# Smaller state products, one read of the new values and a moved fill in the two chunked mixers

## The reference

```python
def step(state, inp):
    u_i, w_i, qk_i, qd_i, kd_i, cd_i = inp
    u = u_i - einsum(w_i, state)                       # the new values
    o = einsum(qd_i, state) + einsum(qk_i, u)          # queries' part, and values' part
    state = state * cd_i + einsum(kd_i, u)             # next state, 64x64 for each head
    return state, o
```

## Time and profile before

| | us |
|---|---|
| median of 3 runs (lowest to highest) | 2084.54 (2083.76 to 2085.15) |
| the profiled execution, its time | 2082.22 |
| its span | 2080.4 |
| PE busy in the span | 1964.4 (94%) |
| DVE / ACT / POOL busy | 916.8 / 473.2 / 869.6 |
| mean granted TensorE clock | 0.973 of full |

### The profile page before, as it was taken

The page is one execution under the profiler, slowest core; times in us unless marked ns, Lnnn a source line. Parts: engine busy times, 40 slices in busy tenths (PEclk is TensorE's granted clock), DMA queues, the critical chain, the costliest instruction groups (busy, mean ns, idle before and its releaser), DMA issues.

```text
span 2080.4 us, 32746 instructions
## 1 busy us (share of the span) xinstructions
PE 1964.4 (94%) x13564; PEld 1566.4 (75%) x13564; DVE 916.8 (44%) x1486; ACT 473.2 (23%) x700; POOL 869.6 (42%) x1100
## 2 busy tenths in 40 slices
PE   4997999998999999999999779899999999999995
PEld 2885777766877878778778568688888888888884
DVE  6456656645444444444443562642232322323325
ACT  4213433342212212122221420521010110101102
POOL 1565422320322223232322257445565555655554
PEclk7999999998999999999999889999999999999998
DMA  7471211212122122120220652011111111111112
GB/s 312 161 235 54 71 50 53 74 74 90 59 63 82 37 85 74 52 90 29 80 74 32 258 192 71 27 35 51 46 46 49 50 50 41 50 50 50 50 41 81
DMA packets 70494, 164.94 MB, mean 79 GB/s; under 512 B 6000, under 2 KB 31088, under 8 KB 70384
## 3 DMA queue, kind: packets, MB, share of 16 engines
q1 hardware_dynamic: 62896, 144.45, 20.9%
q10 hardware_dynamic: 7488, 18.88, 2.4%
HBM read 133.95 MB, written 29.36 MB: 78 GB/s over the span
## 4 chain that ended last, share of the span: by engine, by line
PE 56%; POOL 19%; issue 17%; DMA 3%; DVE 3%; ACT 2%; SPq 1%; POOLq 0%; DVEq 0%; ACTq 0%
PE gbank L540 36%; POOL w_hi L457 9%; POOL w_lo L461 9%; PE mbank L841 3%; PE mbank L612 2%; PE gbank L632 2%; PE gbank L557 1%; DMA fa<-in_w_ada 1%; PE mbank L752 1%; PE mbank L897 1%; PE mbank L931 1%; PE mbank L621 1%; PE gbank L841 1%; PE mbank L908 1%; DMA fa<-mix_scr 1%
## 5 line engine op out<-in xcount | busy, mean ns | idle before, releaser
L457 POOL TENSOR_TENSOR w_hi<-w_raw,zero 128x256 fp32r<-128x256 f32 (+1 forms) x528 | 385.9, 761 | 1131.5 <-PE gbank L540 937.6
L540 PE MATMUL gbank<-h_hi,w_hi 128*128 128x512 f32 x1696 | 675.0, 398 | 10.7 <-POOL w_lo L461 6.9
L540 PE MATMUL gbank<-h_hi,w_lo 128*128 128x512 f32 x1696 | 674.7, 398 | 0.0
L540 PE MATMUL gbank<-h_lo,w_hi 128*128 128x512 f32 x1696 | 670.1, 395 | 0.0
L461 POOL TENSOR_TENSOR w_lo<-w_raw,w_hi 128x256 fp32r<-128x256 f32 (+1 forms) x528 | 444.5, 872 | 10.4
L540 PEld LDWEIGHTS gbank<-h_hi,w_hi 128*128 128x128 f32 x1696 | 320.4, 189 | 92.9 <-issue 20.7
L540 PEld LDWEIGHTS gbank<-h_hi,w_lo 128*128 128x128 f32 x1696 | 320.3, 189 | 70.5 <-issue 3.4
L540 PEld LDWEIGHTS gbank<-h_lo,w_hi 128*128 128x128 f32 x1696 | 320.5, 189 | 67.6 <-issue 3.0
L1056 PE MATMUL mbank<-ra,w_hi 128*128 128x512 f32 x640 | 197.0, 389 | 0.0
L1056 PEld LDWEIGHTS mbank<-ra,w_hi 128*128 128x128 f32 x640 | 120.2, 188 | 24.9
L2066 DVE SCALAR_TENSOR_TENSOR fa<-mbank,mod,fa 128x1024 f32<-128x1024 f32 x40 | 51.3, 1283 | 169.2 <-PE mbank L1056 169.2
(11 more groups left out here) (320 smaller groups left out, 2190.4 us busy)
## 6 DMA issues: line engine op xcount, KB each, us to landing
w_raw<-in_w_tail SPq DMA_DIRECT2D x74, 512.0 KB, 3.6
fa<-in_w_ada SPq DMA_DIRECT2D x48, 512.0 KB, 5.1
w_raw<-in_w_in SPq DMA_DIRECT2D x26, 512.0 KB, 3.7
p_scr<-fa ACTq DMA_DIRECT2D x20, 512.0 KB, 2.6
w_raw<-in_w_mix SPq DMA_DIRECT2D x16, 640.0 KB, 3.9
fa<-in_xT SPq DMA_DIRECT2D x16, 512.0 KB, 7.9
fa<-p_scr SPq DMA_DIRECT2D x8, 1024.0 KB, 5.7
w_raw<-in_w_gate SPq DMA_DIRECT2D x16, 512.0 KB, 4.6
```

Of the source, the lines that this page charges most:

```text
L457: last = pool.tensor_tensor(hi[:, c], raw[:, c], zero[:, 0:1].to_broadcast([P, w]), ALU.add)
L540: mm = pe.matmul(gb[bank], w, r, start=(q == 0), stop=(q == 3 * ks - 1))
```

## The change

The products with state and into state are cut to the 64x64 blocks of each head. The queries' part moves from `to_state` into `from_state`, ahead of the new values. The new values of even and odd heads go to two different banks (mb[2] and mb[1], swapped between the two chunks), and one copy reads both. The products for both next states come ahead of those into y. One more cut of the fill, at 43, stands ahead of `heads(1, gd["ltr"])`, so that 7 of the 12 matmuls that stood ahead of it follow it; and `gated(0)` goes behind `first_blocks` on DVE.

```diff
-FILL_S1 = (10, 22, 38, 50)
+FILL_S1 = (10, 22, 38, 43, 50)
-_SUM = ["rw_s", "rw_Yd", "gd_s", "gd_Yd"]
+_SUM = ["rw_s", "gd_s", "rw_Yd", "gd_Yd"]
...
                 gates(i, FILL_S1[3])
                 pe.wait_ge(sem("gd_ltr"), at("gd_ltr", i))
                 heads(1, gd["ltr"], None, "gd_g6")
+                gates(i, FILL_S1[4])
...
+                def u_bank(e, par_):
+                    return mb[2 if e == par_ else 1]
...
-                    pe.wait_ge(sem(f"{nm}_TT"), at(f"{nm}_TT", i, 5))
-                    heads(1, b_["TT"], rhs, off=off, first=nm == "rw")
+                    pe.wait_ge(sem("gd_TT"), at("gd_TT", i, 5))
+                    for h in range(4):
+                        u_ = 256 + off // 2 + h // 2 * 64
+                        for c in chunks:
+                            pe.matmul(u_bank(h % 2, c.start // 64)[c, u_:u_ + 64], b_["TT"][c, h * 64:h * 64 + 64], rhs[c, h * 64:h * 64 + 64],
+                                      start=nm == "rw" and h < 2, stop=True, skip_group_check=True)
...
                 def from_state(par_):
...
+                    if par_:
+                        pe.wait_ge(sem("gd_Yd"), at("gd_Yd", i, 1))
+                    for nm, st, yb in (("gd", 1, 3), ("rw", 0, 2)):
+                        for t in range(2):
+                            y_ = slice(t * P + 64 * par_, t * P + 64 * par_ + 64)
+                            for r in (0, 64):
+                                q_ = ar_i[r:r + 64, t * 256 + P + 64 * par_:t * 256 + P + 64 * par_ + 64] if nm == "rw" else gd["qd"][r:r + 64, y_]
+                                pe.matmul(mb[yb][r:r + 64, y_], state[r:r + 64, st, t, r:r + 64], q_,
+                                          start=nm == "gd" and par_ == 0 and t == 0, stop=True, skip_group_check=True)
                     for st in range(2):
                         for t in range(2):
-                            w_ = par_ * 256 + st * P + t * 64
-                            last = pe.matmul(mb[1][R, st * 256 + t * P:st * 256 + (t + 1) * P], uw[:, w_:w_ + 64],
-                                             state[:, st, t, :], start=False, stop=True, skip_group_check=True)
+                            w_, u_ = par_ * 256 + st * P + t * 64, 256 + st * P + t * 64
+                            for e, r in enumerate((0, 64)):
+                                last = pe.matmul(u_bank(e, par_)[R, u_:u_ + 64], uw[r:r + 64, w_:w_ + 64], state[r:r + 64, st, t, r:r + 64],
+                                                 start=False, stop=True, skip_group_check=True)
...
                 def to_state(par_):
+                    pe.wait_ge(sem("new_u"), at("new_u", i, par_ + 1))
+                    for nm, terms, s_bank in (("rw", ((rw["tokBK"][R, 0:256], rw["u"]), (rw["tokBK"][R, 256:512], rw["tokVA"])), mb[0]),
+                                              ("gd", ((gd["kd"][R, :], gd["u"]),), gb[1])):
...
+                            for n_, (key, val) in enumerate(terms):
+                                for r in (0, 64):
+                                    hc = slice(t * P + r, t * P + r + 64)
+                                    last = pe.matmul(s_bank[r:r + 64, hc], key[:, hc], val[R, hc], start=n_ == 0,
+                                                     stop=n_ == len(terms) - 1)
+                        last.then_inc(done(f"{nm}_s", i), 1)
+                    for nm, terms, yb in (("rw", ((rw["u"], rw["rbt"]), (rw["tokVA"], rw["rkt"])), 2), ("gd", ((gd["u"], gd["qkt"]),), 3)):
+                        for t in range(2):
                             for lhs, rhs in terms:
+                                for r in (0, 64):
+                                    hc, c = slice(t * P + r, t * P + r + 64), t * P + 64 * par_
+                                    last = pe.matmul(mb[yb][r:r + 64, c:c + 64], lhs[R, hc], rhs[R, hc], start=False, stop=True,
+                                                     skip_group_check=True)
...
-                gated(0)
                 dve.wait_ge(sem("gd_qkt"), at("gd_qkt", i))
                 first_blocks("gd", gd, t64(mb[1][:, 0:256]), "gd_g6", ALU.subtract)
+                gated(0)
...
                 def new_values(par_):
-                    for nm, off in (("rw", 0), ("gd", 256)):
-                        dve.tensor_copy(u_all[R, off:off + 256], mb[1][R, off:off + 256]).then_inc(done(f"{nm}_u", i), 1)
+                    dve.tensor_copy(u_all[R, :].rearrange("p (q e c) -> p e q c", e=2, c=64),
+                                    (mbank[R, 1:3, 256:512] if par_ else mbank[R, 2:0:-1, 256:512]).rearrange("p e (q c) -> p e q c", c=64)).then_inc(done("new_u", i), 1)
```

More of the change, by code:

```diff
@@ L77 @@
                + ["rw_Ym", "gd_Ym", "+rw_gm", "+rw_k2", "rw_TT", "gd_TT"]
-               + ["rw_u", "gd_u", "+rw_bonp"] + ["rw_S"] * 4 + ["gd_S"] * 4
-               + ["+rw_ar", "+rw_ar", "+rw_km", "rw_u", "gd_u", "+rw_bm", "+rw_tl", "+rw_tl"] + ["rw_S"] * 4 + ["gd_S"] * 4
+               + ["new_u", "+rw_bonp"] + ["rw_S"] * 4 + ["gd_S"] * 4
+               + ["+rw_ar", "+rw_ar", "+rw_km", "new_u", "+rw_bm", "+rw_tl", "+rw_tl"] + ["rw_S"] * 4 + ["gd_S"] * 4
                + ["+gd_kn", "+gd_kq", "+gd_dtm", "rw_yc", "gd_o", "rw_o"]),
@@ L914, in to_state @@
                         for t in range(2):
[L915 to L922, removed]
@@ L923, in to_state @@
-                        last.then_inc(done(f"{nm}_s", i), 1)
[L925 to L929, removed]
+                            for n_, (key, val) in enumerate(terms):
[3 more added lines that the diff above has]
+                                                     stop=n_ == len(terms) - 1)
@@ L930, in to_state @@
+                        last.then_inc(done(f"{nm}_s", i), 1)
+                    for nm, terms, yb in (("rw", ((rw["u"], rw["rbt"]), (rw["tokVA"], rw["rkt"])), 2), ("gd", ((gd["u"], gd["qkt"]),), 3)):
+                        for t in range(2):
                             for lhs, rhs in terms:
-                                last = pe.matmul(mb[yb][r:r + 64, c:c + 64], lhs[R, h * 64:h * 64 + 64],
-                                                 rhs[R, h * 64:h * 64 + 64], start=False, stop=True,
-                                                 skip_group_check=True)
+                                for r in (0, 64):
+                                    hc, c = slice(t * P + r, t * P + r + 64), t * P + 64 * par_
+                                    last = pe.matmul(mb[yb][r:r + 64, c:c + 64], lhs[R, hc], rhs[R, hc], start=False, stop=True,
+                                                     skip_group_check=True)
```

## The result

The change took the kernel from 2084.85 to 2037.26 us (medians of 4 runs each; 2034.72 to 2039.29 after): ratio 0.9771, 95% interval 0.9754 to 0.9788, some 47.7 us (44 to 51). The forecast was 2039.3, range 2031 to 2052. The profiled execution took 2039.29, its span 2037.4. That is 43.0 us less than the profiled span before, and not 47.7: this execution was the longest of its four, and its blocks began at 492.3 instead of about 488.8, since ahead of them the clock stood at half for 51.2 us where it was 44.4 in the profile before.

What follows compares the result with a forecast made beforehand. TensorE's queue was taken to bound the blocks. State stage 32.7, fill around T 9.5 and clock 3.0 sum to 45.2 us off the profiled 2082.22, giving 2037.0; plus 2.3 for the median, 2039.3, range 2031 to 2052.

Steps and rivals of the forecast that it cites:

- The queue: Mixer blocks: each is a single queue of TensorE work, so its savings count in full until another engine's result is late.
- The state stage: from_state and to_state: 64x64 records at 0.030 us each save about 2.05 us a half-block, 32.7 us over sixteen halves.
- The shared bank: Query products in from_state: both row halves write one bank on different partitions without going serial; otherwise saving 7 us smaller.
- rival 2: State stage: two row halves block each other in new values or queries, 7.2 us each; 2046.5, both 2053.7; chance 0.08.
- The fill around T: Before the inversion's first level: moved fill saves 1.30 us in seven blocks, 0.4 in block 0; 9.5 us in all.
- The margins of 0.3: Around the first T: ltr and T would each be ready about 0.3 us before PE needs them.
- The one copy: new_values on DVE: one 64x512 copy takes 0.68 us, hidden by fill matmuls before to_state; costs nothing.
- The clock: Mixer blocks: both falls to half clock, 1.5 us each at to_state runs, vanish as the runs shorten; 3.0 us.
- Rival 4: State stage: quarters don't overlap, a 64x64 record costs 0.11 us like the wide one; 2145 us; chance 0.02.

Runs made afterwards that it cites:

- e3: Kernel after with the first-T part undone (cut of the fill at 43 and move of gated(0)), state stage alone: 2047.80 us, ratio 0.9825, 79.55 us a block.
- e5: Kernel after with the query products in from_state as wide as before, at their new place: 2044.94 us, ratio 0.9800.
- e6: Kernel after with the products into the states as wide as before: 2052.16 us, ratio 0.9834.
- e7: Kernel after with the new values' products as wide as before, all in one bank: 2046.98 us, ratio 0.9810.
- e2: Kernel after with gated(0) back ahead of first_blocks on DVE, the cut at 43 kept: 2035.73 us, ratio 0.9771.
- e4: Kernel after with the 10 fill matmuls between from_state(0) and to_state(0) moved behind to_state(0): 2042.11 us, ratio 0.9805.
- e9: Kernel before with only the first-T part (cut of the fill at 43, gated(0) behind first_blocks): 2076.12 us, ratio 0.9957.
- e10: Kernel before, unchanged, run again for a second profile: 2086.61 us.
- e11: Kernel before, unchanged, run once more for a third profile: 2088.59 us.
- e8: Kernel after with to_state's products reordered, all of one array quarter before the other's within each group: 2045.29 us, ratio 0.9806.
- the second measurement: The same two kernels, before and after, unchanged and timed again: 2083.02 to 2038.31 us, ratio 0.9773.

## Why the prediction was right

**The queue.** "What TensorE saves there counts in full": a block lost 5.65 us, and the first T (1.30, e3) and the state stage (4.35) are all of it.

**The state stage, 32.7 forecast.** The step held; its size was 4.35 x 8 = 34.8 in the blocks. from_state came to 1.07 for 1.11 and to_state with the dearer fill ahead to 1.64 for 1.68: the record costs 0.029, at the lower bound, not 0.030. e5 to e7 price its three kinds of product, and L916 shows the one that no row of before had.

**The shared bank** (rival 2) fell: L910 stands at (0.62 - 0.22)/12 = 0.033 or less with both row halves writing one bank on different partitions. Two row halves into one bank on the same partitions weren't tried, so whether the second bank for the new values is needed stays open.

**The fill around T, 9.5 forecast**: 1.30 a block as worked out, 9.5 and 9.6 by time. The margins of 0.3 held (0.35 and 0.34). In blocks 1 to 7 the move of gated(0) was not needed (e2); in block 0 it gave the 0.4 forecast, and 1.4 us of the wait stay there.

**The one copy**: 0.68 as taken from L1834, covered; e4 takes the cover away and finds the price.

**The clock, 3.0 forecast**: right in kind, and shown by e9 to e11; it is nearer 3.5 over several profiles than the 3.0 read from one. The prediction named the length of the run as the reason; the runs show only that the falls go with the old state stage.

**Rival 4** (quarters don't overlap) fell: 24 records of L939 stand 0.028 apart, all in one row half, where e8's single quarter has 0.058. The sum of the measured parts, 34.8 + 9.5 + 3.5 = 47.8, is near the measured 47.7 (interval 44 to 51); that it agrees to 0.1 is luck, with 44.7 in the second measurement. The forecast was 45.2. Luck had a part in the forecast time as well: 2.3 us were added to it because the median before lay above the profiled execution, and after, the median lay 2.0 below.

What failed was an expectation of an experiment: e8's 21 us, since I let each quarter's run end before the next began.

## What to carry to other kernels

In a block where TensorE's queue has no gaps, count starts, not busy time: a product's price is the distance to the next start, and it can be read off another group of the same shape in the same trace. Products with block-diagonal operands, cut into 64x64 pieces that take turns between quarters of the array, cost less although there are twice as many, and one tile shape for neighbouring groups saves the drains between them. A wait at the head of a stage is filled by moving work behind the product that starts the chain, and the margins decide where the cut goes.

## What the runs showed that I had not expected

TensorE starts products out of the program's order: in e8 the other quarter's run began while up to three records of the run before it were still to start, and of an expected 1.35 us a half only 0.43 was lost. And the clock fell behind the old to_state runs although the engine shows no gap in them. The stretch of the kernel before that ends at its fall of 805.4, all of it one to_state run (columns as rows 2):

```profile
802.00:805.40 3.40, 3.40 (x40) 2.95 (x40) 1.12 (x4) 1.07 (x2) 3.20 (x5) 1.00 0.20 77
```

PE is busy in all of its 3.40 us, and the clock fell right behind it all the same. A row that shows the engine fully busy is no sign that the clock will hold.
